# First loads of x and of two weight chunks cut finer, most parameters and one constant loaded behind them, on a one-core transformer kernel

## What is computed

```python
def rms_norm(x, g):
    xf = x.astype(jnp.float32)
    return xf * lax.rsqrt(jnp.mean(xf * xf, -1, keepdims=True) + EPS) * g.astype(jnp.float32)

def even_mixer(h, w_in, ...):
    z = h @ w_in
    u, v, q, k, vb = jnp.split(z, ...)
    ...
    qh = rms_norm(heads(q), q_g)
    kh = rms_norm(heads(k), k_g)
    ...
```

## Time and profile before

| | us |
|---|---|
| runs of the kernel before | 3242.6, 3236.98, 3240.22 (median 3240.22) |
| span of the profiled execution | 3239.6 |
| median less this span | 0.6 |
| PE busy | 3184.8 (98% of the span) |
| ACT busy / DVE busy / POOL busy | 1176.3 / 1177.6 / 1462.8 |
| weight loads | 276 DMAs of 1 MB, and chunk 0 in four of 256 KB |

### The profile page before, as it was taken

How to read it: one execution, slowest core, us unless ns; L and a number is a source line. 1 busy time by engine, 2 the same in 40 slices (tenths; PEclk the granted TensorE clock), 3 DMA queues, 4 the chain that set the end, 5 groups by cost and what they waited for, 6 DMA issues and landing times.

```text
span 3239.6 us, 39346 instructions
## 1 busy us (share of the span) xinstructions
PE 3184.8 (98%) x15820; PEld 2619.2 (81%) x15820; DVE 1177.6 (36%) x1727; ACT 1176.3 (36%) x1388; POOL 1462.8 (45%) x1112
## 2 busy tenths in 40 slices
PE   8999999999999999999999999999999999999998
PEld 7878888888888888888776888888888877788887
DVE  6534431344443112210757522114221366752212
ACT  4544432433433232322427433224322343742322
POOL 4335444433555445445460354454444373054443
PEclk9999999999999999999999999999999999999999
DMA  4212223211222222222320132222222241022222
GB/s 149 79 53 104 104 91 105 108 66 66 92 103 91 104 104 95 99 104 98 128 106 21 54 115 91 104 104 91 91 104 104 78 166 69 14 91 92 102 100 96
DMA packets 46233, 302.55 MB, mean 93 GB/s; under 512 B 5392, under 2 KB 7440, under 8 KB 10784
## 3 DMA queue, kind: packets, MB, share of 16 engines
q1 hardware_dynamic: 41040, 292.79, 25.2%
q10 hardware_dynamic: 5072, 7.96, 0.8%
HBM read 296.54 MB, written 2.10 MB: 92 GB/s over the span
## 4 chain that ended last, share of the span: by engine, by line
issue 46%; POOL 34%; PE 16%; DVE 2%; ACT 1%; DMA 0%; POOLq 0%; ACTq 0%; DVEq 0%; SPq 0%
POOL w_lo L2374 34%; PE main L424 13%; PE main L1902 1%; PE main L566 1%; ACT b_p L2056 0%; DMA stage<-in_w 0%; DVE h_lo L2435 0%; DVE b_p L2278 0%; ACT b_pT L2048 0%; PE misc L484 0%; DVE b_p L2253 0%; DVE y L886 0%; PE main L1707 0%; POOLq L2372 0%; POOLq L97 0%
## 5 line engine op out<-in xcount | busy, mean ns | idle before, releaser
L2374 POOL TENSOR_TENSOR w_lo<-stage,w_hi 128x512 fp32r<-128x512 f32 x1104 | 1457.4, 1354 | 1742.4 <-ACT w_hi L636 1742.4
L424 PE MATMUL main<-h_hi,w_lo 128*128 128x512 f32 x2456 | 962.9, 392 | 3.4 <-POOL w_lo L2374 3.1
L424 PE MATMUL main<-h_hi,w_hi 128*128 128x512 f32 x2456 | 957.5, 390 | 0.0
L424 PE MATMUL main<-h_lo,w_hi 128*128 128x512 f32 x2456 | 957.4, 390 | 0.0
L636 ACT ACTIVATE w_hi<-stage 128x2048 fp32r<-128x2048 f32 x276 | 524.6, 1910 | 417.5 <-DMA stage<-in_w 416.7
L424 PEld LDWEIGHTS main<-h_hi,w_lo 128*128 128x128 f32 x2456 | 462.1, 188 | 105.8 <-issue 7.1
L424 PEld LDWEIGHTS main<-h_hi,w_hi 128*128 128x128 f32 x2456 | 462.0, 188 | 97.1
L424 PEld LDWEIGHTS main<-h_lo,w_hi 128*128 128x128 f32 x2456 | 462.3, 188 | 94.6 <-issue 0.5
L424 PE MATMUL main<-hid_hi,w_lo 128*128 128x512 f32 x1168 | 454.5, 389 | 0.0
L424 PE MATMUL main<-hid_hi,w_hi 128*128 128x512 f32 x1168 | 454.4, 389 | 0.0
L424 PE MATMUL main<-hid_lo,w_hi 128*128 128x512 f32 x1168 | 454.4, 389 | 0.0
(11 more groups left out here) (337 smaller groups left out, 3168.7 us busy)
## 6 DMA issues: line engine op xcount, KB each, us to landing
stage<-in_w SPq DMA_DIRECT2D x276, 1024.0 KB, 4.8
x<-in_xT SPq DMA_DIRECT2D x4, 512.0 KB, 7.8
out_x<-x ACTq DMA_DIRECT2D x4, 512.0 KB, 2.7
stage<-in_w SPq DMA_DIRECT2D x4, 256.0 KB, 8.0
b_r<-sq ACTq DMA_DIRECT2D x4, 256.0 KB, 7.5
b_r<-sq ACTq DMA_DIRECT2D x4, 255.5 KB, 9.4
ev_ws<-in_ev_ws ACTq DMA_DIRECT2D x1, 512.0 KB, 7.4
b_pos<-in_pos ACTq DMA_DIRECT2D x2, 256.0 KB, 2.7
```

Of the source, the lines that this page charges most:

```text
L424: last = pe.matmul(acc[:, m, :], w[a], r[b], start=start and k == 0 and j == 0, stop=stop and k == nk - 1 and j == 2)
L2374: last = e.tensor_tensor(c.w_lo[:, s, k:k + 2, :].rearrange("p k n -> p (k n)"), c.stage[:, s, k * CW:(k + 2) * CW], c.w_hi[:, s, k:k + 2, ...
```

## The change

Everything lies in the first 45 us of the program.

- SP loads x and chunk 0 in 8 parts instead of 4 (one tile of x of 256 KB, rows of 2 KB; an eighth of the chunk of 128 KB, rows of 1 KB), both on one semaphore. Chunk 1 follows in two halves of 512 KB. Only then come the parameters (all but the first 8 columns) and the constant `blockones`, and behind these chunks 2 and 3.
- ACT loads the first 8 columns of the parameters (the gains of the first norm), then `ones`, then `ident`. It no longer loads `blockones`.
- ACT makes a copy of one column first, then per part the tile of `h_hi` and the eighth of `w_hi` (in this order), then chunk 1's `w_hi` in 4 pieces. POOL follows with 8 pieces of 128x256 and 4 of 128x512.
- PE waits per k in chunk 0, and per two k in chunk 1.
- The waits for the whole parameter table move: on ACT to the start of `even_scalar`, on DVE behind `join_banks`, where the halving of the post-norm gains now stands too.
- `even_tensor` is not changed; it waits for the same three constants.

```diff
-PARTS = 4
+PARTS = 8
 PART = CHUNK // PARTS
+HALF = 4
...
+        self.gains_loaded = sem("gains_loaded")
         self.params_loaded = sem("params_loaded")
+        self.w1_part = [sem(f"w1_part{i}") for i in range(2)]
...
 def chunk_products(pe, n, c, acc, hi, lo, nk, k0=0, start=True, stop=True, wait_k=None, mt=2, at={}):
...
-    if n.chunk > 0:
+    if n.chunk > 1:
         pe.wait_ge(c.w_lo_done, n(c.w_lo_done))
     for k in range(nk):
-        if n.chunk == 0 and k % 2 == 0:
-            pe.wait_ge(c.part_lo, k // 2 + 1)
+        if n.chunk == 0:
+            pe.wait_ge(c.part_lo, k + 1)
+        if n.chunk == 1 and k % 2 == 0:
+            pe.wait_ge(c.part_lo, PARTS + k // 2 + 1)
...
 def even_scalar(act, n, c, norm, a, out):
+    act.wait_ge(c.params_loaded, 16)
     act.dma_start(c.ev_mask[:, :], a["ev_mask"]).then_inc(c.mask_loaded, 16)
...
-            sp.dma_start(c.par[:, :], a["par"]).then_inc(c.params_loaded, 16)
...
             for p in range(PARTS):
-                sp.dma_start(two(c.x, p), a["xT"][:, 2 * p:2 * p + 2, :]).then_inc(c.x_part[p], 16)
+                sp.dma_start(tile(c.x, p), a["xT"][:, p, :]).then_inc(c.x_part[p], 16)
                 sp.dma_start(c.stage[:, 0, p * PART:(p + 1) * PART], first[:, p * PART:(p + 1) * PART])\
-                    .then_inc(c.w_part[p], 16)
+                    .then_inc(c.x_part[p], 16)
+            for p in range(2):
+                sp.dma_start(c.stage[:, 1, 4 * p * PART:4 * (p + 1) * PART],
+                             second[:, 4 * p * PART:4 * (p + 1) * PART]).then_inc(c.w1_part[p], 16)
+            sp.dma_start(c.par[:, 8:], a["par"][:, 8:]).then_inc(c.params_loaded, 16)
+            sp.dma_start(c.blockones[:, :], a["blockones"]).then_inc(c.blockones_loaded, 16)
...
         def _(act):
             n = Count()
+            act.dma_start(c.par[:, 0:8], a["par"][:, 0:8]).then_inc(c.gains_loaded, 16)
+            act.dma_start(c.ones[:, :], a["ones"]).then_inc(c.ones_loaded, 16)
             act.dma_start(c.ident[:, :], a["ident"]).then_inc(c.ident_loaded, 16)
-            act.dma_start(c.blockones[:, :], a["blockones"]).then_inc(c.blockones_loaded, 16)
-            act.dma_start(c.ones[:, :], a["ones"]).then_inc(c.ones_loaded, 16)
-            act.wait_ge(c.params_loaded, 16)
...
     act.wait_ge(c.eps_ready, 1)
-    split_next(act, n, c)
+    act.activation(c.stat[:, 13:14], c.eps, ACT.Copy)
+    act.wait_ge(c.gains_loaded, 16)
+    for k in range(PARTS):
+        act.wait_ge(c.x_part[k], 32)
+        col = PC["norm"] + norm * 8 + k
+        act.activation(c.h_hi[:, k, :], c.x[:, k, :], ACT.Copy, scale=c.par[:, col:col + 1])\
+            .then_inc(c.h_hi_done, 1)
+        act.activation(c.w_hi[:, 0, k, :], c.stage[:, 0, k * PART:(k + 1) * PART], ACT.Copy).then_inc(c.part_hi, 1)
+    for p in range(HALF):
+        if p % 2 == 0:
+            act.wait_ge(c.w1_part[p // 2], 16)
+        act.activation(c.w_hi[:, 1, 2 * p:2 * p + 2, :].rearrange("p k n -> p (k n)"),
+                       c.stage[:, 1, 2 * p * PART:2 * (p + 1) * PART], ACT.Copy).then_inc(c.part_hi, 1)
+    n.chunk += 2
```

More of the change, by code:

```diff
@@ L252, in sem @@
             return ctx.enter_context(nc.semaphore(name))
+        self.gains_loaded = sem("gains_loaded")
         self.params_loaded = sem("params_loaded")
+        self.w1_part = [sem(f"w1_part{i}") for i in range(2)]
         self.x_part = [sem(f"x_part{i}") for i in range(PARTS)]
-        self.w_part = [sem(f"w_part{i}") for i in range(PARTS)]
         self.part_hi = sem("part_hi")
@@ L2340, in _ @@
             n = Count()
-            sp.dma_start(c.par[:, :], a["par"]).then_inc(c.params_loaded, 16)
             first = a["w"][0:1, :, :].rearrange("o p n -> (o p) n")
+            second = a["w"][1:2, :, :].rearrange("o p n -> (o p) n")
             for p in range(PARTS):
-                sp.dma_start(two(c.x, p), a["xT"][:, 2 * p:2 * p + 2, :]).then_inc(c.x_part[p], 16)
+                sp.dma_start(tile(c.x, p), a["xT"][:, p, :]).then_inc(c.x_part[p], 16)
                 sp.dma_start(c.stage[:, 0, p * PART:(p + 1) * PART], first[:, p * PART:(p + 1) * PART])\
-                    .then_inc(c.w_part[p], 16)
+                    .then_inc(c.x_part[p], 16)
[4 more added lines that the diff above has]
+            sp.dma_start(c.blockones[:, :], a["blockones"]).then_inc(c.blockones_loaded, 16)
             def load(e, chunk, s, first):
-                if first and s == 0:
+                if first and s < 2:
                     return
@@ L2365, in low_part @@
                         e.wait_ge(c.part_hi, p + 1)
+                        e.tensor_tensor(c.w_lo[:, 0, p, :], c.stage[:, 0, p * PART:(p + 1) * PART],
+                                        c.w_hi[:, 0, p, :].bitcast(F32), ALU.subtract).then_inc(c.part_lo, 1)
+                    return
+                if first and s == 1:
+                    for p in range(HALF):
+                        e.wait_ge(c.part_hi, PARTS + p + 1)
                         k = slice(2 * p, 2 * p + 2)
-                        e.tensor_tensor(c.w_lo[:, 0, k, :].rearrange("p k n -> p (k n)"),
-                                        c.stage[:, 0, p * PART:(p + 1) * PART],
-                                        c.w_hi[:, 0, k, :].rearrange("p k n -> p (k n)").bitcast(F32),
+                        e.tensor_tensor(c.w_lo[:, 1, k, :].rearrange("p k n -> p (k n)"),
+                                        c.stage[:, 1, 2 * p * PART:2 * (p + 1) * PART],
+                                        c.w_hi[:, 1, k, :].rearrange("p k n -> p (k n)").bitcast(F32),
                                         ALU.subtract).then_inc(c.part_lo, 1)
@@ L2399, in _ @@
             n = Count()
[L2400 to L2405, removed]
             dve.memset(c.eps, EPS).then_inc(c.eps_ready, 1)
+            dve.wait_ge(c.gains_loaded, 16)
             for kind, kw in plan:
@@ L2411, in first_scalar @@
 def first_scalar(act, n, c, norm, a, out):
[L2412 to L2421, removed]
-    act.wait_ge(c.eps_ready, 1)
-    split_next(act, n, c)
+    act.wait_ge(c.eps_ready, 1)
+    act.activation(c.stat[:, 13:14], c.eps, ACT.Copy)
[6 more added lines that the diff above has]
+        act.activation(c.w_hi[:, 0, k, :], c.stage[:, 0, k * PART:(k + 1) * PART], ACT.Copy).then_inc(c.part_hi, 1)
+    for p in range(HALF):
+        if p % 2 == 0:
[3 more added lines that the diff above has]
+    n.chunk += 2
     for m, t in enumerate((c.acc, c.sq, c.val, c.sq)):
@@ L2439, in first_vector @@
     join_banks(dve, n, c)
+    dve.wait_ge(c.params_loaded, 16)
+    for l in range(2):
+        for f in (0, 2):
+            at = PC["post"] + 8 * (3 * l + f)
+            dve.tensor_scalar(c.par[:, at:at + 8], c.par[:, at:at + 8], 0.5, None, ALU.mult)
 def ffn_tensor(pe, n, c, conv, norm, post):
```

## The result

The changed kernel takes 3244.57 us (median of 20 runs, 3240.77 to 3249.19), against 3240.5 us for the kernel before (median of 20, 3236.03 to 3245.7). The ratio is 1.0013, with a 95% interval from 1.0007 to 1.0019: slower by about 4 us, and by less than the 0.2% that the prediction set as a bound. The profiled execution has a span of 3243.1 us and a time of its own of 3245.26 us.

The account below looks back on a forecast made before the run. PE, busy for 98% of the span, bounds the kernel. PE's start +9.4, wait inside chunk 0 −0.2, pause −2.4, clock −1.7 give 5.1 later; 3239.6 + 5.1 + 0.6 = 3245.3 us, range 3241.5 to 3249.

Parts of the forecast that it names:

- What decides: At PE's start: PE still waits for `blockones`, now twentieth on SP's queue; start of PE +9.4 us.
- Landing at 17.7: SP's queue: `blockones` lands at 16.4 + 1.3 = 17.7 us, with bounds 16.9 and 20.0.
- The terms for the finer loads of x and chunk 0: SP's queue: 8 DMAs instead of 4 cost +0.6 us for x and +0.5 for chunk 0.
- The picture of an even queue: SP's queue: x and weight parts land every 1.1 us, 0.70 + 0.41 for each of 8 pairs.
- First product 3.4 later: PE's start: small matmuls take 3.43 us as before, so the first product comes at 21.1.
- Chunk 0 in 11.8: PE in chunk 0: 11.8 us instead of 12.0, the operands lying ready; end at 32.9.
- No pause, no low clock: PE before and in chunk 1: pause gone, −2.4 us, and low clock behind it gone, −1.7.
- `h_lo` at 1.28 us each: DVE in chunk 0: 1.28 us per `h_lo`, the last done by about 17, before PE begins.
- the third: PE's start: PE isn't held, starts between 6.5 and 8.3; −4.3 up to −6.1 us, 3234 to 3236; chance 0.07.
- the first: SP's queue: `blockones` lands later still, at the bound 20.0; +7.4 us, 3247.6; chance 0.18.
- The second, the clock: PE's early chunks: without the earlier low clock in timed runs +6.8, 3247.0; with an earlier rise 3244.6; chance 0.17.
- The fourth, a gain: PE's start and later program: the change gains as meant and more, over 0.2% (6.5 us) faster; chance 0.03.

Follow-up runs that it names:

- e1: Changed kernel, but PE waits for `blockones` at its first use instead of at its start: 3234.56 us, 0.9983 of the kernel before.
- e2: Changed kernel with `blockones` loaded by ACT again, fourth on its queue, the wait still at PE's start: 3234.09 us, 0.9983 of the kernel before.
- e3: Kernel before with only the load of `blockones` moved to SP, behind chunk 1: 3245.85 us, 1.0019 of the kernel before.
- e6: e1 without the 8 small matmuls at PE's start: 3233.54 us, 0.998 of the kernel before.
- e8: e1 without ACT's copy ahead of the data: 3234.82 us in one run.
- e7: e1 with x and chunk 0 loaded in 4 DMAs each, still worked in 8 parts: 3235.87 us, repeated 3238.72, one run each.
- e5: Kernel before with only chunk 1 rounded, split and waited for in four pieces, its load one DMA: 3236.84 us, 0.9988 of the kernel before.
- e9: Kernel before with x and chunk 0 loaded in 8 DMAs each, waited for in the same four pairs: 3240.43 us in one run.
- e4: Changed kernel with `blockones` issued on SP's queue behind chunk 2 instead of ahead of it: 3246.92 us, 1.0025 of the kernel before.

## Why the prediction was right, step by step

- **What decides.** Shown by e1, e2 and e3: the wait for `blockones` at PE's start is the loss. Taken away, the change gains 5.5 us of the median; put alone into the kernel before, it costs as much as the whole change.
- **Landing at 17.7.** Measured 18.2 and 17.7, and 17.2 to 17.4 in e1, e6 and e8. The total came out right, but by two errors that cancel. The terms for the finer loads of x and chunk 0, +1.1 us together, were too large: with coarse loads and all else equal `blockones` landed at 17.0 and 16.9 (e7 and its repetition), which leaves 0.6 in the mean, and no run shows the 0.41 for a DMA of 1 KB rows. The base was low: chunk 1, at 16.4 in the profile that the sum used, landed at 16.8 in the second profile of the kernel before (5.74 + 11.1), and `blockones` behind it at 17.0 in e3. The picture of an even queue failed too: pairs of parts were to land every 1.1 us, and came, from 4.3 (1.20 + 3.1) to 14.8 (8.59 + 6.2), every 1.5. In a stretch of the first microseconds the queue was slow, and then made up for it. Two stretches of the DMA view of the changed kernel show it, 4 to 9 us and 11 to 14 us:

```profile
DMA packets 1014, 1.27 MB, mean 254 GB/s; under 512 B 117, under 2 KB 624, under 8 KB 1014
...
DMA packets 773, 1.15 MB, mean 384 GB/s; under 512 B 86, under 2 KB 438, under 8 KB 773
```

 The kernel before has a slow start as well, 300 GB/s and 433 GB/s in the same two stretches, so that most of it was contained in the 16.4. Counting from a landing that holds the same bytes was the safe way.
- **First product 3.4 later**: 21.64 − 18.24 = 3.40. **Chunk 0 in 11.8**: 33.07 − 21.64 = 11.43. The clock rose by 22.62, 4.4 us behind PE's start, where the sum took 4.9 from the kernel before. So chunk 0 gave back 0.4 of the 0.5 us by which the landing was late.
- **No pause, no low clock**: so it was. Forecast for chunk 1 was 32.9, measured 33.07, and the sum of 5.1 us is 5.18 at chunk 2. That it fits so closely is luck: the −1.7 for the clock belongs to the one profile that the sum was read from. Between the second profiles the kernel before doesn't pay it, and PE is 6.43 later.
- **`h_lo` at 1.28 us each**: it took 0.75 to 0.92, since the 1.28 held waits for POOL (below), and the last was done at 16.5, before PE began. This lay under PE's wait, as did the finer pieces and the copy ahead of the data.
- **The time.** Forecast 3245.3, measured 3244.57. The difference of the medians is 4.1 us, and its interval goes from 2.3 to 6.2, so the timed runs can't tell it from the 5.18 of chunk 2. About 0.4 of it doesn't lie in the span at all, which the forecast didn't have: the time of an execution is 1.7 to 1.9 us above its span in the kernel before, e3, e5 and e9, and 2.1 to 2.3 in the changed kernel and all its relatives. The spans of the two profiles differ by 3.5 only. The clock falls equally often behind chunk 2 in both, but at other places: from 670 to 690 us the granted clock is 0.91 in the kernel before and 1.00 in the changed one, from 690 to 730 it is 1.00 and 0.96. What is shorter is PE's waiting at one line of the second block, before and after:

```profile
PE main L1707 <- issue: 6.2, 2, 3.3
...
PE main L1707 <- POOL w_lo L2374: 3.8, 2, 2.1
```

```profile
PE main L1712 <- issue: 4.6, 2, 2.5
...
PE main L1712 <- POOL w_lo L2390: 2.3, 2, 1.7
```

 This is 10.0 us against 6.9. The same line takes 5.7 to 10.0 in the fourteen profiles: 5.7 in e7, where PE starts early, and 8.6 in e4, where it starts latest. So a late start of PE doesn't by itself make it short. What sets it was not settled.
- **The rivals.** PE was held at its start, against the third. The bound of the first, a landing at 20.0, wasn't reached; e4 shows what it would have brought (19.80: 1.0025). The second, the clock, is real: the second profile of the kernel before has no fall behind the pause. How often it falls there in the timed runs isn't recorded; a loss of 6.8 us, as without any fall, lies outside the interval. The fourth, a gain, is out: the interval lies above 1.
- **The page's rule on small DMAs** (the Trainium skill, DMA: Bandwidth & Descriptors, Bandwidth), taken as a floor of 0.95 us for each of the eight 128 KB parts, would have put the landing at 22.0. The trace disagrees: 18.2. The page's figure is for single transfers of 64 KB that GpSimd issues, so this speaks against its use as a floor in a filled queue of SP, not against the page.

## What to carry to other kernels

A load that is moved behind others takes along every wait that names it, also one that stands far ahead of the first use. Before moving a "small" constant out of the way, search for its semaphore, and put the wait at the first reader. Cutting loads finer pays only where the next whole piece doesn't take the gain back: here the parts of chunk 0 alone brought nothing, chunk 1 in pieces 3 us, and both with the wait in its place 5.5 us, faster than either kernel (0.9983).

## What the runs showed of the hardware

- **Two queues get about equal numbers of rows, and so the length of the rows decides who waits.** A 64 KB constant third on ACT's queue took 7.6 and 7.8 us to land beside loads with 2 and 4 KB rows on SP's queue, and 3.7 to 4.5 beside 1 and 2 KB rows. Its own size and place were the same. In the kernel before it took 6.6, and 3.5 with the finer loads (e9). From 3 to 5 us of e7 the queues moved 200 and 198 rows. With the rows the size of a DMA was halved too; no run separates the two, but the counts of rows speak for the rows. How many rows make a turn isn't shown.
- **DVE waits for POOL's instruction in progress.** In the changed kernel the four tiny instructions that halve the gains stand beside POOL's split of chunk 2, and two of the four take 1.26 us, each to the end of POOL's instruction in progress. The rows give shortest, median and longest duration in ns, for the changed kernel:

```profile
L2458 DVE TENSOR_SCALAR par<-par x4: 159/709/1260, 26.0 to 28.4; 128x8 f32<-128x8 f32 x4
```

 and in the kernel before, where POOL had nothing to do yet:

```profile
L2405 DVE TENSOR_SCALAR par<-par x4: 165/165/172, 3.6 to 3.9; 128x8 f32<-128x8 f32 x4
```

 The same holds for `h_lo`, first in the kernel before and then in the changed one:

```profile
L2435 DVE SCALAR_TENSOR_TENSOR h_lo<-x,par,h_hi x8: 739/1518/1834, 10.3 to 18.7; 128x512 fp32r<-128x512 f32 x8
```

```profile
L2448 DVE SCALAR_TENSOR_TENSOR h_lo<-x,par,h_hi x8: 750/752/916, 5.2 to 15.5; 128x512 fp32r<-128x512 f32 x8
```

 It takes 0.74 us alone, and up to 1.83 where an instruction of POOL of 1.3 us is in progress: the one that starts at 13.19, beside POOL's from 13.18 to 14.47, ends at 15.02, 0.55 behind it. In the changed kernel the `h_lo` of a part starts ahead of POOL's piece of that part, and pays at most 0.17 for the end of the piece ahead. The Trainium skill (SBUF — State Buffer, Who interferes with whom) says that the two engines share a pair of ports that is locked for a whole instruction and not divided; these rows agree.
- **The small matmuls bring the clock up.** In e6, without them, the first eight distances of products are 0.42 to 0.56 us, and from 10.36 on 0.23; in e1, with them, PE started at 6.36 and the products follow at 0.31 and less from 9.60 on.
